# Moving two side lanes by three steps: the output rows' lane and the preparation's lane of a two-layer block on one core

## What is computed

```python
def _layer(x, ctx, c, c_ctx, ..., update_ctx):            # called twice, update_ctx = (l == 0)
    h_lat = x * (1.0 + scale[:, None]) + shift[:, None]
    h_ctx = ctx * (1.0 + scale_c) + shift_c
    ... = jnp.split(h_lat @ w_in, SPLIT_POINTS, axis=-1)  # 29 rows of 128 features
    ... = jnp.split(h_ctx @ w_in, SPLIT_POINTS, axis=-1)
    rin_l = _rwkv_inputs(ru_l, *rwkv_params)              # conv, decay, kk, kd, bd: "the preparation"
    S_f, S_b, ys_c = _rwkv_bidir(rin_c, S0, S0)
    _, _, ys_l = _rwkv_bidir(rin_l, S_f, S_b)             # the scan, both directions
    yr_l = _rwkv_output(ys_l, rin_l, r_k, gn_g, gn_b, x.dtype)   # group norm of the rows, bonus
    gk_l = _apply_axial_rope(gk_l, cos, sin)              # norm and rope of q and k
    gq_l = _apply_axial_rope(gqa_q(aq_l), cos, sin)
    ya_l = _block_attention(gq_l..., keys, vals)          # 6 query heads over 2 key heads
    yn_l = _neighbourhood_attention(nq_l..., rpb)         # banded, with bias and masks
    y_l = jnp.concatenate([yr_l * silu(rg_l), ya_l * silu(ag_l), yn_l * silu(ng_l)]) @ w_out
    x = _layer_norm(DEEPNORM_ALPHA * x + gate[:, None] * y_l, ln_g, ln_b)
```

## Time and profile before

| | us |
|---|---|
| median of three runs | 4791.81 (4785.33 to 4795.76) |
| the profiled execution | 4786.9 |
| its span on the core | 4785.1 |
| PE busy | 4509.2 of it (94%) |
| DVE, ACT, POOL busy | 2688.2, 1465.5, 975.9 |

### The profile page before, as it was taken

The page is one execution under the profiler, slowest core; times in us unless marked ns, Lnnn a source line. Parts: engine busy times, 40 slices in busy tenths (PEclk is TensorE's granted clock), DMA queues, the critical chain, the costliest instruction groups (busy, mean ns, idle before and its releaser), DMA issues. The chain is left out here.

```text
span 4785.1 us, 96335 instructions
## 1 busy us (share of the span) xinstructions
PE 4509.2 (94%) x40786; PEld 2857.7 (60%) x40786; DVE 2688.2 (56%) x4592; ACT 1465.5 (31%) x2452; POOL 975.9 (20%) x1169
## 2 busy tenths in 40 slices
PE   9998989899999999998999988999999799989898
PEld 4446855444444445554999855664444499976663
DVE  5753476785432236755545356567586545446656
ACT  2212453100000113332233255543243232326552
POOL 0002211000100000001232243540000232315460
PEclk9999999999999999999999999999999999989999
DMA  4331012443425543444211110313354411111122
GB/s 135 107 99 67 33 63 75 132 141 114 166 72 176 180 145 118 170 164 144 59 56 55 32 47 34 96 58 97 127 192 169 150 50 49 56 33 50 51 73 84
DMA packets 341465, 468.66 MB, mean 98 GB/s; under 512 B 39559, under 2 KB 244647, under 8 KB 340080
## 3 DMA queue, kind: packets, MB, share of 16 engines
q1 hardware_dynamic: 289216, 266.26, 17.9%
q0 software_dynamic: 51824, 196.24, 11.7%
HBM read 328.14 MB, written 147.86 MB: 99 GB/s over the span
## 5 line engine op out<-in xcount | busy, mean ns | idle before, releaser
L491 PE MATMUL psum<-arena 128*128 128x512 f32 x2352 | 1025.1, 592 | 2.2 <-issue 1.0
L3291 PE MATMUL psum<-arena 64*64 64x64 f32 (+6 forms) x22800 | 899.9, 232 | 34.0 <-POOLq L222 16.1
L3291 PEld LDWEIGHTS psum<-arena 64*64 64x64 f32 (+3 forms) x22800 | 861.3, 144 | 74.5 <-issue 20.9
L491 PEld LDWEIGHTS psum<-arena 128*128 128x128 f32 x2352 | 444.1, 189 | 544.3 <-issue 538.5
L1078 PE MATMUL psum<-arena 128*128 128x512 f32 x1344 | 583.8, 595 | 11.4 <-DVEq L222 5.3
L706 PE MATMUL psum<-arena 128*128 128x512 f32 x1232 | 535.9, 595 | 4.3 <-DVE arena L772 2.4
L2676 DVE CUSTOM_DVE_ANT_0 arena<-psum,arena 128x512 f32<-128x512 f32 (+3 forms) x532 | 292.8, 589 | 315.6 <-PE psum L2563 298.4
L1078 PEld LDWEIGHTS psum<-arena 128*128 128x128 f32 x1344 | 254.8, 191 | 330.8 <-issue 320.1
L706 PEld LDWEIGHTS psum<-arena 128*128 128x128 f32 x1232 | 232.3, 190 | 301.3 <-issue 291.7
L3497 DVE TENSOR_TENSOR arena<-arena,psum 128x384 f32<-128x384 f32 x320 | 177.9, 556 | 322.7 <-PE psum L3291 289.9
L2563 PE MATMUL psum<-arena 64*128 64x512 f32 (+3 forms) x1192 | 273.3, 544 | 87.1 <-DVE arena L2676 64.0
(11 more groups left out here) (346 smaller groups left out, 5194.6 us busy)
## 6 DMA issues: line engine op xcount, KB each, us to landing
arena<-w_in SPq DMA_DIRECT2D x86, 512.0 KB, 5.6
proj<-arena SPq DMA_DIRECT2D x172, 256.0 KB, 2.1
arena<-w_mod POOLq DMA_DIRECT2D x24, 1024.0 KB, 5.7
arena<-down_sum SPq DMA_DIRECT2D x40, 512.0 KB, 3.6
arena<-proj POOLq DMA_DIRECT2D x31, 640.0 KB, 5.3
arena<-proj SPq DMA_DIRECT2D x28, 640.0 KB, 6.8
arena<-w_down SPq DMA_DIRECT2D x30, 512.0 KB, 3.7
x_home<-arena POOLq DMA_DIRECT2D x26, 512.0 KB, 5.1
```

What stands on the lines that cost most here:

```text
L491: ins = pe.matmul(ps[:, b, :], L[:, k, :], R[:, k, :], start=(p in ("P1", "P5", "P6", "P7") and k == 0), stop=(k == KT // 2 - 1), skip_gro ...
L3291: return pe.matmul(out, lhsT, rhs, start=first, stop=last, skip_group_check=not (first and last))
```

## The change

`RwkvOut` gets a number of leading steps in which it does nothing (3 in the first of the two layers, none in the last), behind POOL's first DMAs. In the first layer `gqa` then takes one side step in each of its first three steps and two in every other; in the last layer it takes three at every sixth step and two in the others. In both layers the projection takes its side steps at n = 8, 9 and 10 too, which were pauses; the pauses at n = 16 to 19 stay.

```diff
-    def __init__(self, core, room, y, bonus, gate, mix, par, lo=0):
+    def __init__(self, core, room, y, bonus, gate, mix, par, lo=0, lead=0):
...
-        self.lo = lo
+        self.lo, self.lead = lo, lead
...
-        self.steps = 16 * RT
+        self.steps = lead + 16 * RT
+
+    def leading(self):
+        for _ in range(self.lead):
+            yield
...
         directions(0)
         others(0)
+        yield from self.leading()
...
-        gemm.pace = lambda n: n < 8 or 11 <= n < 16 or n >= 20
+        gemm.pace = lambda n: n < 16 or n >= 20
...
-        out = RwkvOut(core.lanes[1], Room((0, 8192)), y_dir, rw["bonus"], proj[10 * P:13 * P, :], h, par, lo=CTX if last else 0)
+        out = RwkvOut(core.lanes[1], Room((0, 8192)), y_dir, rw["bonus"], proj[10 * P:13 * P, :], h, par, lo=CTX if last else 0, lead=0 if last else 3)
         gqa.beside = [out]
-        gqa.pace = lambda n: 2
+        gqa.pace = lambda n, last=last: 2 + (n % 6 == 2) if last else 1 + (n > 2)
```

## The result

| | before | after |
|---|---|---|
| median of 12 runs each, us | 4786.8 (4783.39 to 4795.76) | 4802.47 (4793.21 to 4805.83) |
| ratio, 95% interval | | 1.0028 (1.0019 to 1.0036) |
| profiled execution, us | 4786.9 | 4805.47 |
| its span | 4785.1 | 4803.7 |

What follows compares the result with a forecast made beforehand. PE was taken to bound the projections (busy 489.3 of 492.9 and 438.1 of 450.2 us). Terms 3.9 + 4.6 - 1.8 - 3.1 - 3.2 - 9 + 2.4 - 7.5 = -13.7 us gave 4778 us, range 4766 to 4792.

Steps and rivals of the forecast that it cites:

- The opening: Start of the projections' preparation lane: moving it three steps earlier costs 0, up to 4 us per layer if loads are late.
- PE waits in the opening: Sign that the forecast is wrong: PE waiting at n = 11 to 16 of the projection.
- Second pass: Last layer's preparation, units without context columns: PE waits sum to 4.7 us against 0.8 before, so +3.9 us.
- slower rival: DVE falls behind in all six preparation passes, 28 us of waits instead of 4.7, time 4802 us; chance 8%.
- `GqaPrep`: K preparation in the projections: waits and low clock cost +4.6 us in the last layer, -1.8 us in the first.
- The ends: Projection ends: wait behind falls to 3.7 us, a new meeting wait costs 1.2 (0.4 to 2); net -3.1 and -3.2 us.
- The clock: Half-speed matmuls charged where the trace had shown them: 4.8 us in the last layer's `GqaPrep`, 3.2 before.
- First `gqa`: First layer's `gqa`: the 8.66 us hole at its start goes and scores come earlier; -9 us, between -3 and -13.
- one bound of the first `gqa`: First layer's `gqa`: matmuls staying at half speed at the start put the scores' gain at its 12.0 us end.
- Last `gqa`: Last layer's `gqa`: denser units with lane steps falling together cost +2.4 us, bounds 0 to 5.
- The term for units 14 and 20 together: Last layer's `gqa`: denser lane steps in these two units cost 1.1 us together, less what goes.
- The masks: Last layer's `na`: masks land before the stage starts, so POOL waits 0.24 us instead of 7.70; -7.5 us.

Runs made afterwards that it cites:

- e1: Kernel before plus only the projections' lane steps at n = 8 to 10, both layers; 4808.3 us against 4789.46, ratio 1.0037.
- e4: Changed kernel with PE's wait for the low-rank weights and tanh'd row moved just ahead of its first use; 4791.21 us, ratio 1.0006 to the kernel before.
- e5: Changed kernel with PE's tanh wait moved later and six empty steps instead of two before `GqaPrep`'s meeting; 4777.75 us, ratio 0.9979 to the kernel before.
- e2: Kernel before plus only the first layer's `gqa` part (three leading empty steps, one lane step in each of the first three); 4778.47 us, ratio 0.9979.
- e3: Kernel before plus only the last layer's `gqa` part (three lane steps at n = 2, 8, 14, 20); 4788.88 us, ratio 0.9996.
- e6: Changed kernel with the last `gqa`'s third steps at n = 2, 3, 9 and 10; 4794.3 us, ratio 1.0014 to the kernel before.
- e7: Changed kernel, last `gqa`'s third steps at n = 2, 3, 9, 10, last projection's old pace, six empty steps before `GqaPrep`'s meeting; 4762.14 us, ratio 0.9947 to kernel before.

## Why the prediction was wrong, point by point

**The opening: wrong, and the main miss.** The prediction put the price at 0 because "PE's first lane wait is at n = 15". I had taken for it the first wait ahead of a lane matmul, and passed over the two waits that stand alone at lane step 3. Before, they lay at n = 14, three products (10.4 us) later, and cost nothing: the last tanh row of ACT ended at 3381.77 + 1.27 = 3383.0, and PE, whose products at n = 12 to 14 began at 3376.2, came there at about 3386.6:

```profile
3381.77 1.27 ACT L2921 ACTIVATE arena<-arena 64x1280 f32<-64x1280 f32 x1
```

At n = 11 the tanh is 5.85 us too late. With the low clock behind (9.56 for 7.03 us) that is 8.4 us in e1's and the changed kernel's last projection. The prediction had named just this as a sign against it ("PE waits in the opening"), and had even reckoned that ACT would wait 2 to 5 us for its row. In the first layer the same wait cost nothing. The context columns at n = 3 and at n = 11 take 7 us each there instead of 3.6, so PE comes to the product at n = 12 only at 1799.8, 37.9 us behind its first context columns (31.1 in the last layer), and ACT's tanh (in the changed kernel) ended at 1798.1:

```profile
1796.84 1.27 ACT L2921 ACTIVATE arena<-arena 64x1280 f32<-64x1280 f32 x1
```

So that layer had 1.7 us to spare. The "up to 4 us in each layer" was a bound on the loads and not on this chain, and too low. The opening alone doesn't make up the miss: with it mended (e4) the ratio is 1.0006, where 0.9971 was forecast.

**Second pass: right.** Forecast 4.7 us in waits of 1.3, 1.0, 0.2 and 2.2; measured 1.49, 0.78 and 1.99, in all 4.26, the same in e1, e4 and e5. The slower rival, that S3 is late in all six passes, is refuted: no such wait stands in the other passes. That its 4802 us is the time that was measured is chance.

**`GqaPrep`: right.** Last layer, forecast 3.6, 0.2, 4.0, 0.6, 0.6, 4.9; measured 3.67, 0.18, 4.04, 0.61 and 4.80, and 0.47 for the drain behind the first rotation in e1. The low clock behind these waits was put at 4.8 us and is 0.8 + 2.2 + 1.8 = 4.8. First layer, forecast 1.4 in all, measured 0.18 + 0.61 + 0.61.

**The ends: half right.** The wait behind the product is 3.72 and 3.71 us, as forecast. The meeting ahead of it was taken at 1.2 and measured 3.42 and 3.13, above its own upper bound of 2. In the changed kernel the last product also takes 8.84 and 8.81 us for 7.03. So -3.1 and -3.2 became +0.9 and +0.5: 3.4 + 3.7 + 1.8 against 8.0, and 3.1 + 3.7 + 1.8 against 8.1. The chain to the meeting came as it was reckoned: the rope operations end at 3790.0, the last `kx` copy is issued at 3793.0 and lands 9.0 us later, at about 3802.0. But PE goes on only at 3803.89. These 1.9 us from the landing to PE's next matmul, the meeting itself, stood in no term of the sum, and with the 1.2 they make the 3.1. e5 shows the -4.3 that was there to be had.

**The clock: the second miss.** The sum charged slow matmuls only where the earlier trace rows had shown them, 1.6 us in all for the last projection. Measured are 8.8. The rows above account for most: 2.5 behind the opening, 0.4 in the second pass, 0.8, 2.2 and 1.8 for `GqaPrep`'s matmuls less 3.2 that was there before, 0.5 and 1.8 for products behind them. So a wait added on PE can cost more than its length: here 10.7 us of idle time came with 8.8 us of slower matmuls. The Trainium skill (TensorE: Matmul & The Clock Gate, Part 1) says that the throttled state is the default and activity releases it; the trace agrees, in 9.56 us for 7.03 behind 5.85 us of standing still. The prediction had used that rule for one bound of the first `gqa` and for nothing else.

**First `gqa`: right.** Forecast -9, measured -10.1 in the changed kernel, -7.5 in e2's profile and -11 by e2's medians. The 8.66 us ahead of `RwkvOut`'s first matmul are gone; the lane's first wait is now 2.27 us at 23.2 us from the start:

```profile
2772.33 3.11 PE L3567 MATMUL psum<-arena 128*128 128x512 f32 x4 [2.27 <-DVE arena L3622]
```

The Trainium skill (GPSIMD Engine Reference, Specifications), which states that POOL's SBUF interfaces are shared with VectorE's operations on two SBUF inputs, had spoken for less than 9. Against what the prediction took, the lane's first addition meets no sum of POOL's; it takes 1.49 us as before. The centring behind it (L3625, which was L3617) meets one, in DVE's and POOL's rows:

```profile
2785.52 2.10 DVE L3625 TENSOR_TENSOR arena<-arena 128x1280 f32<-128x1280 f32 x1 [2.06 <-ACT arena L3598]
```
```profile
2786.42 1.70 POOL L2537 TENSOR_TENSOR arena<-arena 128x256 f32<-128x256 f32 x1
```

The trace agrees with the page: the centring took 1.49 us before, and POOL's sum takes 0.64 where it is alone. That is 0.6 us on DVE, too little to be seen in the 10.1.

**Last `gqa`: the size was off.** Forecast +2.4, bounds 0 to 5; e3 alone has +6.4, 5.0 of it idle time. The term for units 14 and 20 together, 1.1 us, is the one mis-sized: where step 0 joins steps 14 and 15, DVE is busy for 5.2 us in a row (4450.38 to 4455.6) and PE waits 2.65 and 2.12 us in e3 (3.06 and 2.12 in the changed kernel), with matmuls at half speed behind it. e6 places the steps otherwise and has +3.3. Of the changed kernel's 11.7 us, another 3.6 stand in the opening of the stage, where e1 has them too, without this part of the change, and e6 has not, with the same projection ahead. The waits there are the same in all three (1.6, 1.5, 2.6, 1.5 and 1.5 us); the matmuls are slower. What decides it stays open.

**The masks: right.** Forecast -7.5, measured -8.3 in e3. POOL starts the biased tables (L3914) without a DMA wait, 0.24 us behind its memsets as forecast from the earlier trace rows:

```profile
4564.24 3.19 POOL L2505 MEMSET arena<- 128x896 f32 x4
4567.67 6.01 POOL L3914 TENSOR_TENSOR arena<-arena 128x640 f32<-128x640 f32 x4 [0.24 <-issue]
```

**The sum.** Forecast -13.7, by the profiles +18.6. The 32.3 us between them: the last projection 14.2, the last `gqa` 9.3, the first projection 4.0, and 4.4 ahead of all that was changed, 2.2 in the last scan, less 1.1 in the first `gqa` and 0.8 in the masks. By the runs of its parts (1.0037, 0.9979, 0.9996) the change would be at 1.0012, and it measured 1.0028 (1.0019 to 1.0036). Each part's interval is 0.0009 to 0.0013 wide on either side, so the difference may be chance; whether the parts make each other worse was not settled. The chances gave "slower" 6%. They were drawn from rivals that all took the list of PE's waits as complete. What failed in the prediction, then, is first the 0 for PE in the opening (it was 8.4 us), next the clock behind added waits (8.8 us in the last projection for 1.6), the 1.2 for the meeting (3.4 and 3.1), and the 2.4 for the last `gqa` (6.4 alone).

## What to carry to other kernels

When a side lane is moved earlier, list every wait in each engine's lane program with its new place, also the ones that stand apart from the operation that uses the result; set a wait directly ahead of its first use, and a meeting behind the main work's last piece. An empty step in a lane can be the time that a load or a chain of three engines needs, as here in the opening: find the chain's end in the trace before the step is taken away. And place a denser step by what falls into its unit, not by an even pattern: the same 48 steps, ended in the same unit, cost 3.3 us in e6 and e7 and 6.4 in e3.

## What the runs showed of the hardware

The same wait doesn't always bring the low clock. Ahead of the first projection's last product PE stood still for 3.42 us in the changed kernel and for 3.32 us in e4:

```profile
2249.39 8.84 PE L491 MATMUL psum<-arena 128*128 128x512 f32 x16 [3.42 <-POOLq L222]
```
```profile
2243.66 7.14 PE L491 MATMUL psum<-arena 128*128 128x512 f32 x16 [3.32 <-POOLq L222]
```

The product behind took 8.84 us in the one and 7.14 in the other. The first layer's scan, with the same instructions in every kernel, shows the same on a larger scale; these are the windows of the kernel before and of e7:

```profile
2258.47:2745.54 487.07, 477.48 (x11700) 456.54 (x11700) 228.16 (x461) 138.91 (x320) 145.51 (x162) 0.97 0.20 58
```
```profile
2252.71:2735.17 482.46, 470.27 (x11700) 449.52 (x11700) 228.26 (x461) 138.90 (x320) 145.52 (x162) 0.99 0.20 59
```

11700 matmuls took 477.5 us at a granted clock of 0.97 and 470.3 at 0.99. Nothing in the kernels says which it will be, and it moves a single profile by 5 us. That is as much as several of the terms that were summed here.
